# Tokens scattered into rows grouped by expert, transposed on VectorE, four weight buffers, second gate once per token on GpSimd

## What is computed

```python
    expert_idx = grp[:, None] * EXPERTS_PER_GROUP + top_i
    comb = jnp.sum(jax.nn.one_hot(expert_idx, N_EXPERTS, dtype=f32) * (top_p * p_grp)[..., None], axis=1).astype(x.dtype)
    y = jnp.zeros_like(x)
    for e in range(N_EXPERTS):
        a, u = jnp.split(x @ w_gu[e], 2, axis=-1)
        y = y + comb[:, e:e + 1] * ((jax.nn.silu(a) * u) @ w_dn[e])
...
        xs = xs + g2 * hierarchical_moe(h, *moe_w)
...
    y_sample = rmsnorm(xs, final_norm)
```

## Time and profile before

| | |
|---|---|
| time, median of 3 runs | 737.27 us (735.97 to 741.42) |
| the profiled execution | 740.09 us, of which the profile's span 738.3 us |
| TensorE busy | 663.9 us (90%), 2710 matmuls |
| VectorE / ScalarE / GpSimd busy | 347.7 (47%) / 180.5 (24%) / 142.8 us (19%) |
| DMA | 138.96 MB, 188 GB/s over the span |
| chain that ended last | 80% of it on TensorE, 8% VectorE, 4% DMA |

### The profile page before, as it was taken

The page is one execution under the profiler, slowest core; times in us unless marked ns, Lnnn a source line. Parts: engine busy times, 40 slices in busy tenths (PEclk is TensorE's granted clock), DMA queues, the critical chain, the costliest instruction groups (busy, mean ns, idle before and its releaser), DMA issues.

```text
span 738.3 us, 7844 instructions
## 1 busy us (share of the span) xinstructions
PE 663.9 (90%) x2710; PEld 366.9 (50%) x2710; DVE 347.7 (47%) x777; ACT 180.5 (24%) x446; POOL 142.8 (19%) x152
## 2 busy tenths in 40 slices
PE   3799999999999999999999999974999999999920
PEld 3344474345556655677777544532444444444410
DVE  3305461431666572475656177787213322233248
ACT  6000200001222211166566322210112211221123
POOL 1042100121103110113223100001033312332062
PEclk9699999999999999999999999995999999999965
DMA  8978833904113040210003396002699999999258
GB/s 284 387 205 305 322 124 123 363 1 142 44 58 100 15 157 0 100 73 1 1 1 115 143 334 264 28 30 87 238 363 362 348 347 354 359 370 346 95 208 332
DMA packets 63347, 138.96 MB, mean 188 GB/s; under 512 B 4710, under 2 KB 11230, under 8 KB 63316
## 3 DMA queue, kind: packets, MB, share of 16 engines
q1 hardware_dynamic: 52344, 109.81, 42.2%
q0 software_dynamic: 5568, 16.68, 6.4%
q10 hardware_dynamic: 5404, 12.06, 4.1%
HBM read 123.76 MB, written 14.74 MB: 188 GB/s over the span
## 4 chain that ended last, share of the span: by engine, by line
PE 80%; DVE 8%; DMA 4%; issue 4%; ACT 2%; SPq 1%; ACTq 1%; POOL 1%; DVEq 0%; POOLq 0%
PE PS L1599 23%; PE PS L1981 15%; PE PS L1996 7%; PE PS L1832 6%; PE PS L1591 5%; PE PS L1747 5%; PE PS L1819 2%; PE PS L1630 2%; DMA PR<-in_w_ada 2%; DMA PR<-scratch_mod 1%; PE PS L1540 1%; PE PS L1726 1%; PE PS L1776 1%; PE PS L1974 1%; PE PS L1803 1%
## 5 line engine op out<-in xcount | busy, mean ns | idle before, releaser
L1599 PE MATMUL PS<-RING,hT 128*128 128x512 f32 x400 | 181.8, 603 | 0.8 <-DVE hT L1037 0.8
L1599 PEld LDWEIGHTS PS<-RING,hT 128*128 128x128 f32 x400 | 74.0, 193 | 87.2 <-issue 86.2
L1981 PE MATMUL PS<-PR,RING 128*128 128x512 f32 x256 | 113.9, 598 | 0.2 <-DVE RING L1454 0.2
L1981 PEld LDWEIGHTS PS<-PR,RING 128*128 128x128 f32 x256 | 47.7, 191 | 55.6 <-issue 53.8
L1832 PE MATMUL PS<-RING,hT 128*128 128x512 f32 x160 | 73.2, 601 | 0.0
L663 POOL TENSOR_TENSOR RING<-RING,PR 128x1024 f32<-128x1024 f32 x16 | 38.0, 2373 | 130.2 <-ACT RING L955 122.6
L1996 PE MATMUL PS<-PR,RING 128*128 128x512 f32 x128 | 57.6, 592 | 0.0
L1459 DVE SCALAR_TENSOR_TENSOR RING<-RING,HM,PS 128x256 f32<-128x256 f32 x16 | 7.7, 481 | 77.8 <-ACT RING L950 77.8
L1832 PEld LDWEIGHTS PS<-RING,hT 128*128 128x128 f32 x160 | 28.8, 190 | 29.6 <-issue 29.5
L1747 PE MATMUL PS<-RING,hT 128*128 128x256 f32 x160 | 36.9, 384 | 0.7 <-ACT TMP L865 0.6
L1591 PE MATMUL PS<-hT,RING 128*128 128x512 f32 (+3 forms) x128 | 37.1, 450 | 0.0
(11 more groups left out here) (339 smaller groups left out, 921.4 us busy)
## 6 DMA issues: line engine op xcount, KB each, us to landing
PR<-in_w_gate_up SPq DMA_DIRECT2D x16, 2048.0 KB, 10.2
PR<-in_w_ada SPq DMA_DIRECT2D x20, 1024.0 KB, 10.8
PR<-in_w_down SPq DMA_DIRECT2D x16, 1024.0 KB, 10.9
RING<-in_w_in SPq DMA_DIRECT2D x14, 1024.0 KB, 7.5
scratch_y<-RING ACTq DMA_DIRECT2D x16, 512.0 KB, 7.4
RING<-in_w_out SPq DMA_DIRECT2D x4, 1024.0 KB, 6.3
TMP<-scratch_gfr SPq DMA_DIRECT2D x10, 256.0 KB, 7.6
scratch_h<-HM SPq DMA_DIRECT2D x5, 512.0 KB, 3.5
```

Of the source, the lines that this page charges most:

```text
L1599: last = mm(PS[:, bank, :], hTv[:, k, t * P:(t + 1) * P], ring[:, ci % 2, k, :], start=(k == 0), stop=(k == KD - 1))
L1981: last = mm(PS[:, 4 + b, :], xgT[:, b, k, :], gub[b][:, k, :], start=(k == 0), stop=(k == KD - 1))
```

## The change

- **Scatter in place of lists.** The lists, `rmat`, `slot_ids`, `place_id` and `place_slot` go. An added row in `ranks` gives each token its place plus 640 times its expert, so that it is at once a row of a scratch `xs` of 16 x 640 rows. GpSimd scatters each `h2` tile there by two indirect DMAs. `h2` has three buffers.
- **Zeroing.** Rows of `xs` that no token fills must hold numbers, so ScalarE's queue writes 16 times 640 rows of 4 KB of zeros (42 MB in all), eight of these DMAs at the mLSTM steps 2 to 9 and eight at the attention units 0 to 7. The zeros come from the tile `fnorm`, cleared by GpSimd. SyncE waits for all of it before it loads `final_norm`.
- **Loading and transposing.** A tile of 128 tokens is loaded by four DMAs to 32 partitions each, in rows of 1 KB, and one VectorE transpose (in blocks of 32 x 32) gives `xgT`. The order within the width that comes out fits weights whose rows are read as `(p k)`, 16 KB (gate-up) or 8 KB (down) in one piece per partition, where before they were read as `(k p)`, in rows of 2 KB and 4 KB. The transposes of `hid` read every second column.
- **Four buffers** for weights and tokens. Two more experts are loaded ahead of the loop.
- **Gates.** The token's weight and the second gate are left out of the loop. Results go over the experts' own input rows in `xs`. After the loop ScalarE scales the first result row, VectorE adds the second times its weight, GpSimd multiplies by the gate (in the order of its program after all ten gathers), VectorE adds to `x1`.
- All rounds run first and the output is made once.

```diff
+        def load_x(s, row):
+            for q in range(4):
+                src = scratch["xs"][bass.ds(row, P), 256 * q:256 * q + 256]
+                sp.dma_start(xq[32 * q:32 * q + 32, s], src.rearrange("(c j) f -> j c f", j=32)).then_inc(xq_in[s], 16)
...
+        sp.wait_ge(h2_sent[0], 64)
+        sp.wait_ge(h2_sent[1], 64)
+        sp.wait_ge(h2_sent[2], 32)
+        for s in range(2):
+            load_x(s, s * T)
...
+        with sp.Fori(1, n_rounds * QUADS) as qd:
+            quad = qd % QUADS
+            for s0 in (0, 2):
+                for s in (s0, s0 + 1):
+                    sp.wait_ge(gu_done[s], qd + 1)
+                    load_x(s, quad * (4 * T - 32) + qd * 32 + s * T)
...
+        for t in range(NT):
+            pool.wait_ge(slot_ready, t + 1)
+            pool.wait_ge(h2_ready, 2 * (t + 1))
+            for j in range(2):
+                pool.indirect_dma_start(out=scratch["xs"], in_=h2[t % 3], in_offset=None,
...
+        for t in range(NT):
+            pool.wait_ge(pick_in[t], 32)
+            pool.wait_ge(y_mixed, t + 1)
+            nc.gpsimd.tensor_tensor(ygate[:, t], ypick[t][1], g2b[:, min(t, 1)], ALU.mult).then_inc(y_gated, 1)
...
+            dst = scratch["xs"][e * T:(e + 1) * T, :].rearrange("(c p) f -> p c f", p=P)
+            act.dma_start(dst, fnorm[:].unsqueeze(1).broadcast_to([P, NT, D])).then_inc(xs_zeroed, 16)
...
+                for t_ in ((0, 1) if t == 0 else range(t + 1, min(t + 2, NT))):
+                    act.wait_ge(pick_in[t_], 32)
+                    nc.scalar.activation(ypick[t_][0], ypick[t_][0], ACT.Copy, scale=cw[:, 0, t_:t_ + 1]).then_inc(y_scaled, 1)
+                act.wait_ge(y_sum, t + 1)
...
+                    dve.wait_ge(xq_in[s], qd * 64 + 64)
+                    dve.wait_ge(gu_done[(s + 2) % 4], qd + (s2 + 1))
+                    V.transpose(xgT[:, b].rearrange("p k (c j) -> p c k j", c=4),
+                                xq[:, s].rearrange("p c (j k) -> p c k j", k=KD)).then_inc(xgT_ready, 1)
...
+        mix_y(0)
+        for t in range(NT + 1):
+            if t + 1 < NT:
+                mix_y(t + 1)
+            if t < NT:
+                dve.wait_ge(y_gated, t + 1)
+                V.tensor_tensor(x1[:, t], x1[:, t], ygate[:, t], ALU.add).then_inc(y_sum, 1)
+            if t >= 1:
+                dve.wait_ge(fin_rstd, t)
...
+            mm(PS[:, 7, NE * t:NE * t + NE], masksb[:, 3, :], erowb[:], start=True, stop=False)
```

More of the change, by code:

```diff
@@ L526, in _ @@
+        sp.wait_ge(outs, 16 * (5 + NT))
     @block.gpsimd
@@ L1405, in _ @@
                 route(t - 1)
-                place_id(t - 2)
             if t == NT - 1:
-                place_slot(t - 2)
-                place_rank(t - 1)
+                place(t - 1)
             residual(t, 1)
@@ L1419, in _ @@
             modulate(t)
-            if 2 <= t < NT - 1:
-                place_slot(t - 2)
-        place_id(NT - 2)
         route(NT - 1)
-        place_rank(NT - 1)
+        place(NT - 1)
+        dve.wait_ge(count_done, 1)
         step(V.tensor_reduce(cnt[:, 0:1], PS[:, 6, 80:96], AX.X, ALU.max))
```

494 lines of the change are left out of this document (170 added, 324 removed).

## The result

The changed kernel takes 754.54 us (median of 4 runs, 751.43 to 760.94) against 737.27 us before: ratio 1.0243, 95% interval 1.0202 to 1.0284. It is slower, and outside the range of the forecast (738.6, 728.5 to 750). The profiled execution took 751.43 us, its span is 749.6 us. The same kernel again gave 752.9 us (750.35 to 759.95), ratio 1.0239 (1.0182 to 1.0297), beside 736.95 us for the kernel before. Medians and ranges here hold all runs of a kernel; its ratio leaves out runs that lie over 1.5% above its fastest.

A forecast was written before the change was run, and what follows sets the result against it. The prediction took TensorE to set the loop, with data close behind. Its terms, -16.9 - 0.3 + 4 + 14.5 = +1.3 us, on the median of 737.27 gave 738.6 us, 8-in-10 range 728.5 to 750.

The forecast's parts named there:

- Zeroing: Zero writes in the mLSTM and attention: +4 us together, bounds 0 and +12.
- each holds ScalarE's queue for an issue: mLSTM: eight zeroing DMAs of 6.4 us each cost ScalarE's queue only their issues, +0.5 us for the first.
- The loop: Expert loop: transposes and the bank wait leave TensorE, seven gaps of 2.42 us saved, -16.9 us.
- The second cover: Loop: a pair's data may take 24.7 us before TensorE waits; taken as 22.9 us, so covered.
- rival 3: Loop bound by data from 24.7 us per pair: 743.6 us at 25.5, 752.4 at 27; chance 0.08.
- The rule weighed there: Loop's token loads: transfers to 32 partitions run at half rate, giving 25.5 us per pair, sum 5 us higher.
- From routing to the first gate-up: Stage between routing and loop: -0.3 us together, bounds -3.5 and +3.
- clock term: Around the first gate-up: products at half speed on TensorE's clock cost 2.2 us where 0.7 was lost before, +1.5.
- After the loop: Stage behind the loop: first gather -1.5 us, added chain +16.0, together +14.5 us, bounds +11 and +22.
- 1.75 + 0.35 (output DMA) + 1.06 + 1.28 + 1.22 = 5.7 us per tile: After the loop, second tile on: square and root, output DMA, scaling, mix, add; 5.7 us where 3.6 held.
- Rival 2: After the loop: VectorE and GpSimd serialize, +22 us in place of +14.5, giving 746.1 us; chance 0.12.
- the queue's stall: Attention: zeroing holds ScalarE's queue, 3.5 us taken; as a rival +12 for zeroing's +4, 746.6 us, chance 0.13.

The follow-up runs named there:

- pitch128: Changed kernel with 128 rows per expert in place of 640, so each zeroing DMA writes 0.5 MB in place of 2.6: 741.18 us.
- zero_early: Changed kernel with the mLSTM's eight zeroing DMAs issued earlier, during the projection, reading zeros from 64 partitions: 788.08 us.
- after: The changed kernel, first measurement and profile, against the kernel before: 754.54 us, ratio 1.0243.
- after_again: The changed kernel unchanged, run again for a second profile: 752.9 us, ratio 1.0239.
- zero_spread: Changed kernel with attention's eight zeroing DMAs at every second unit (0 to 14) in place of units 0 to 7: 750.75 us.
- scales_first: Changed kernel with ScalarE's five scalings of the first results all ahead of its first square and root: 745.56 us (one run).
- gate_dve: Changed kernel with the gate product after the loop done by VectorE in place of GpSimd: 753.49 us (one run).
- gate_dve_scales_first: Changed kernel with the gate product on VectorE and all five ScalarE scalings ahead of its first root: 745.0 us.
- before_zero: Kernel before the change plus only the sixteen zeroing DMAs (42 MB), into a scratch that nothing reads: 752.83 us, ratio 1.0213.

## Why the prediction was wrong

**Zeroing** (+4 forecast, +14.5 in the stages, +15.4 alone): this is the step that failed most. In attention the working was of the right kind, ScalarE's queue running out of room, and its size was within reach: 3.5 forecast, 5.5 measured. In the mLSTM the failure is in "each holds ScalarE's queue for an issue [...] I take +0.5 for the first one". The DMA was costed by the engine that issues it, and the text named the 6.4 us of data each brings without asking what else is on the DMA engines then. SyncE's loads of the mask tiles are, and the pair that TensorE's chain hangs on went from 8.0 to 17.7 us. Their wait reaches TensorE through GpSimd and ScalarE, in one step, which holds 8.5 of the 9.0 us. Zeros with the same issues and a fifth of the data cost 0.5 us there (pitch128), which is the term the forecast had. That it is these loads that carry the delay was read from the chain and the landing times, and it holds in zero_early too, where the zeros have left this stretch, the pair lands in 8.6 us and the 8.5 us are gone; no run changed the mask loads alone.

**The loop** (-16.9 forecast, -10.9 measured, -7 to -15 over the executions of the same loop): TensorE's part was right to 0.1 us per pair (21.15 forecast, 21.06). VectorE's transpose took 2.02 us of the 1.23 to 2.26 that were given, and was covered. The second cover was too thin. The step says that a pair's data may take 24.7 us, which is 340 GB/s for 8.39 MB, and takes 22.9 us (366 GB/s) for its price. The runs put the edge between 353 and 362 GB/s, 23.8 and 23.2 us per pair, so the room was overrated by 0.9 to 1.5 us per pair; the price was about right on average, and the measured 345 to 371 GB/s lie on both sides of that edge. Why the room is smaller is only argued: in the first 30 us of the changed kernel's loop the rate is 310 GB/s, and loads take 24 to 27 us from issue to landing, which the working, an average over the loop, left out. The two ingredients of the price were both seen: long rows bring (338 GB/s without them, in one execution, 345 to 371 with them), narrow token loads take (398 without them). So rival 3 with its 25.5 us, 5 us lost, is about what happened: the seven profiled executions with 640 rows and the changed kernel's loads (after, after_again, zero_spread, zero_early, scales_first, gate_dve, gate_dve_scales_first) average 174.5, which is 4.6 above 169.9, with about 0.6 of it in the first pair's clock.

The rule weighed there, that a transfer to 32 partitions reaches half of the ports (the Trainium skill, *SBUF — State Buffer*, "Door 1: The DMA port swizzle"), gave this case. The trace agrees with it: for about 4 us from 523.7 on, when hardly anything but token pieces was under way in the changed kernel, 158 to 246 GB/s moved with the DMA engines full, though in rows of 1 KB, which may count as well; the zeros from partitions 64 to 127, in rows of 4 KB, moved at 207.

**From routing to the first gate-up** (-0.3 forecast, -2.2 to -3.2 measured over the ten kernels that have the changed code here, bounds -3.5 and +3): the sign was right. The forecast's clock term, +1.5, falls behind the first gate-up product and so into the loop's row of the table: the first pair loses 1.7 us to the clock in after and 3.1 in after_again, where it lost 0.6 before. From the last one-hot sum (505.65) to the first gate-up (518.86) it is 13.2 us against 12.9 before, as the working has it ("nothing gained or lost"). The gain is ahead of that sum: 3.0 us where 1.8 was given.

**After the loop** (+14.5 forecast, +18.0 measured): the first gather came 2.3 us earlier (1.5 forecast). GpSimd's first product began 13.2 us behind it (13.1), and the first `x1` was done at 18.9 (17.0 to 19.3). The failed term is "1.75 + 0.35 (output DMA) + 1.06 + 1.28 + 1.22 = 5.7 us per tile". The round doesn't go through the square and root, which are done early; it goes through VectorE's last product, for which the output DMA waits, and that product is held by GpSimd's: 1.28 + 1.22 + 3.37 + 0.35 + 1.15, with small overlaps and gaps 7.38. Taking GpSimd's product away leaves 6.87 with a VectorE product of some 1.2 in it, so 5.7 for the rest: the term came out right without the lock, by another path. Rival 2 (22 for 14.5) thus happened by half. It had been given 0.12, with "the chain waits on ScalarE between, so there is room" against it. The room was ahead of the mix, and GpSimd starts with the end of the mix, which is also when VectorE starts its two other operations.

**The sum.** Zeroing +10.5 over the forecast, loop +6.0, after the loop +3.5, routing -2.3: 17.7 over +1.3, which is the +19.0 of the stages. With the clock's 1.5 put where it falls, the loop is +4.5 over and the routing -0.8. No single rival gives this: the loop's data wait came nearly in full, the serializing by half, a part of the queue's stall too, and the largest term, the mLSTM's 8.5 us over its 0.5, stood in none of them. The range took each rival alone.

## What to carry to other kernels

A DMA costs three things that must be looked up apart: the issuing queue's time, the queue's room, and its data time on the 16 engines that all queues share. For the last, list every small load that something waits for while it runs, with the slack of each: of the late mask loads here one pair cost 8.5 us and another nothing. Fire-and-forget writes are not free because nobody waits for them. Where a stage stands at 97% DMA share, a faster compute side turns into a data wait, and a few per cent of rate decide how much of the gain is left. When an elementwise product moves from the loop's shadow to the end, first write down the round of the new chain in the order of each engine's program, output DMAs included, and see which two engines work at once on SBUF in it.

## What was not expected of the hardware

- A queue's room: with 2.62 MB per DMA in 4 KB rows, issues took 0.38 us until several were on the way, then up to 4.5 us each (after, before_zero), with landings up to 23.8 us.
- Reading from 64 partitions (64 to 127) halves the rate: 207 GB/s against 419.
- One wait of TensorE is followed by slower products: after 6.0 us eight products took 2.06 us, not 0.89; after 2.12 us 24 took 12.23, not 10.30, with a granted clock of 0.68 from 671 to 675 us.
- While GpSimd multiplies 128x1024, a VectorE product of 1.28 us takes 3.37 and GpSimd's own goes from 2.3 to 3.20 us.
- The same loop, with the same loads, ran at 345 to 371 GB/s from one execution to the next, and its length went with it (179.1 to 171.1 us). The kernel before, whose pairs are longer, varied less: 733.26 to 741.42 us over all its runs, against 736.28 to 749.61 for pitch128.
